# A two-layer transformer backbone on one core: the first and joining stages in another order, and a fourth size of expert, 65 to 96 rows

## The reference

```python
s_lat, s_ctx = silu(c), silu(c_ctx)
for layer in range(2):
    mod_l = split((s_lat @ ada_w[layer] + ada_b[layer]), 6)      # ada_w: 1024 x 6144, 25 MB a layer
    mod_c = split((s_ctx @ ada_w[layer] + ada_b[layer]), 6)
    hl = rmsnorm(xl, norm_g[layer, 0]) * (1 + mod_l[1]) + mod_l[0]   # hc likewise, with mod_c
    # layer 0: ab_mixer, h @ w_in (1024 x 3072), retention on four heads and a gated recurrence, @ w_out
    # layer 1: mla_mixer, latent attention of 16 heads
    xl = xl + mod_l[2] * ol
    tokens = rmsnorm(xl, norm_g[layer, 1]) * (1 + mod_l[4]) + mod_l[3]
    # router: one group of four, two of its eight experts; in layer 0 for all 768 tokens, in layer 1 for 512
    y = sum over the two experts e of  weight_e * ((silu(t @ w_gate[e]) * (t @ w_up[e])) @ w_down[e])
    xl = xl + mod_l[5] * y                                       # xc likewise, layer 0 only
return rmsnorm(xl, final_norm_g)
```

## Time and profile before

| | us |
|---|---|
| median of 3 runs | 2185.58 (2184.8 to 2187.6) |
| the profiled execution, own time | 2187.3 |
| its span in the profile | 2185.6 |
| PE busy | 1713.1 (78%) |
| DVE, ACT, POOL busy | 705.5, 435.5, 259.8 (32, 20, 12%) |
| mean granted TensorE clock | 0.899 |

### The profile page before, as it was taken

The page is one execution under the profiler, slowest core; times in us unless marked ns, Lnnn a source line. Parts: engine busy times, 40 slices in busy tenths (PEclk is TensorE's granted clock), DMA queues, the critical chain, the costliest instruction groups (busy, mean ns, idle before and its releaser), DMA issues. The chain is left out here.

```text
span 2185.6 us, 25873 instructions
## 1 busy us (share of the span) xinstructions
PE 1713.1 (78%) x9070; PEld 895.1 (41%) x9071; DVE 705.5 (32%) x1254; ACT 435.5 (20%) x802; POOL 259.8 (12%) x350
## 2 busy tenths in 40 slices
PE   5999999799499789998614899999938789855651
PEld 2443344645244334444303545555434334433330
DVE  2403675633311111112136227776331111111114
ACT  3102323311001110111113114554101101111112
POOL 1002350301100000001013110000111000000001
PEclk8999999899599999999865899999958999987885
DMA  9767653500799999999963002000169999999993
GB/s 320 239 246 250 217 175 120 199 26 39 315 385 361 413 418 412 424 398 403 419 269 123 2 0 87 1 1 8 54 254 389 414 410 406 413 413 410 414 413 137
DMA packets 105452, 568.10 MB, mean 260 GB/s; under 512 B 22728, under 2 KB 40904, under 8 KB 65568
## 3 DMA queue, kind: packets, MB, share of 16 engines
q1 hardware_dynamic: 90544, 521.94, 60.5%
q0 software_dynamic: 7744, 26.22, 3.4%
q10 hardware_dynamic: 7088, 18.92, 2.2%
HBM read 525.55 MB, written 41.50 MB: 259 GB/s over the span
## 5 line engine op out<-in xcount | busy, mean ns | idle before, releaser
L1927 PE MATMUL exp_gps<-moew_wg,all_hT 128*64 128x512 f32 (+1 forms) x480 | 238.6, 621 | 35.4 <-DMA moew_wu<-in_moe_w_up 33.1
L1921 PE MATMUL exp_gps<-moew_wg,all_hT 128*32 128x256 f32 x1088 | 160.5, 460 | 104.3 <-DMA moew_wu<-in_moe_w_up 97.9
L1928 PE MATMUL exp_ups<-moew_wu,all_hT 128*64 128x512 f32 (+1 forms) x480 | 237.3, 618 | 0.0
L583 PE MATMUL abp_ps<-ab_w,all_hT 128*128 128x512 f32 x384 | 169.6, 597 | 0.6 <-PE abp_ps L587 0.3
L1921 PE MATMUL exp_ups<-moew_wu,all_hT 128*32 128x256 f32 x1088 | 160.2, 460 | 0.0
L1921 PEld LDWEIGHTS exp_gps<-moew_wg,all_hT 128*32 128x32 f32 x1088 | 79.1, 131 | 182.5 <-issue 139.0
L1927 PEld LDWEIGHTS exp_gps<-moew_wg,all_hT 128*64 128x64 f32 (+1 forms) x480 | 77.7, 166 | 169.7 <-issue 169.7
L1955 PE MATMUL exp_yps<-moew_wd,all_hT 128*64 128x512 f32 (+1 forms) x240 | 117.3, 606 | 20.4 <-issue 20.4
L2047 DVE TENSOR_TENSOR all_hT<-all_hT,exp_ups 64x512 f32<-64x512 f32 (+1 forms) x30 | 20.7, 690 | 343.6 <-ACT all_hT L1997 343.6
L1957 PE MATMUL exp_yps<-moew_wd,all_hT 128*64 128x512 f32 (+1 forms) x240 | 116.8, 603 | 0.0
L583 PEld LDWEIGHTS abp_ps<-ab_w,all_hT 128*128 128x128 f32 x384 | 71.6, 190 | 98.5 <-issue 98.3
(11 more groups left out here) (399 smaller groups left out, 2572.0 us busy)
## 6 DMA issues: line engine op xcount, KB each, us to landing
moew_wg<-in_moe_w_gate SPq DMA_DIRECT2D x64, 2048.0 KB, 24.7
moew_wu<-in_moe_w_up SPq DMA_DIRECT2D x64, 2048.0 KB, 30.0
moew_wd<-in_moe_w_down SPq DMA_DIRECT2D x64, 2048.0 KB, 31.3
all_X<-in_ada_w SPq DMA_DIRECT2D x40, 1024.0 KB, 6.2
ab_w<-in_ab_w_in SPq DMA_DIRECT2D x6, 2048.0 KB, 9.1
ys<-abp_zero SPq DMA_DIRECT2D x32, 384.0 KB, 7.1
ys<-exp_y ACTq DMA_DIRECT2D x13, 512.0 KB, 8.7
ab_rows<-in_ada_w SPq DMA_DIRECT2D x6, 1024.0 KB, 12.0
```

Of the source, the lines that this page charges most:

```text
L583: last = nc.tensor.matmul(ps[i % RB][:], hT[:, kk, what * P:(what + 1) * P], w[n % S][:, kk, :], start=(kk == 0), stop=(kk == KD - 1))
L1921: last = nc.tensor.matmul(bank[lo + j * Q:lo + (j + 1) * Q, 0:HC], x[:, k, 0:Q], wt[:, k, j * HC:(j + 1) * HC], start=(k == 0), stop=(k == ...
L1927: nc.tensor.matmul(gps[0:rows, :], x[:, k, 0:rows], w.g[q][:, k, :], start=(k == 0), stop=(k == KD - 1))
L1928: last = nc.tensor.matmul(ups[at:at + rows, :], x[:, k, 0:rows], w.u[q][:, k, :], start=(k == 0), stop=(k == KD - 1))
```

## The change

It has three parts; nothing else is touched.

**The first stage** (`ab_project`). The six loads of rows go to the head of SP's queue, ahead of the chunks. The gains, convolution weights and biases, gate biases and lambdas come as 52 contiguous rows of 128 values (`laid`, five loads on ACT's queue); PE transposes them once and DVE copies them to columns (`pcols`). Block 0 is issued ahead of the tables. The transposes of the tiles stand behind earlier chunks. The ring has three buffers, and its uses move from two, two, two, one and one behind consecutive groups to one, two, two, two and one.

**The joining stage** of layer 0 is a new function, `combine_into_mla`: ACT scales the rows into `xn`, PE transposes them, ACT copies to `hT`, and gain and shift are applied to `hT` by columns, odd channels by ACT, even by DVE. POOL only issues gathers. Its modulation comes as five sets of eight rows (`laid`), transposed by PE. `combine` stays for the end of layer 1.

**The experts** get a form for 65 to 96 rows (`T3`): 64 rows in column halves and 32 rows in four column groups, each step with both. The 32 rows' gate and up are in a bank `qps`, their product in `h2`, their y in the bank `hps`. Gathers and stores of such an expert move 96 rows. The waits of PE for the copies of y (`y_act`, `y_dve`) stand, for all forms, ahead of the transposes of h and no longer behind them.

```diff
-        RING = 2
+        RING = 3
...
-        ADA_AT = [2 + 7 * r + r // 4 + at for r in range(ROUNDS - 1) for at in (0, 0, 1, 1, 2, 2, 3, 4)]
+        ADA_AT = [2 + 7 * r + r // 4 + at for r in range(ROUNDS - 1) for at in (0, 1, 1, 2, 2, 3, 3, 4)]
...
+            load_rows(sp, c, a, x_in)
             for kk in range(KD):
                 ada_chunk(0, kk, ada_first[kk], first_ready[kk])
+            block_of(0)
             tables.sync(sp)
-            block_of(0)
             block_of(1)
-            for t in range(CONV):
-                sp.dma_start(cw[:, t, :], a["lru_conv_w"][0, t].rearrange("(c p) -> p c", p=P),
-                             allow_slow_non_contiguous=True).then_inc(p_ready, 16)
-            sp.dma_start(cw[:, CONV, :], a["lru_conv_b"][0].rearrange("(c p) -> p c", p=P),
-                         allow_slow_non_contiguous=True).then_inc(p_ready, 16)
-            for dg in range(4):
-                sp.dma_start(gb[:, dg, :], a["lru_gate_b"][0, dg // 2, dg % 2].rearrange("(c p) -> p c", p=P),
-                             allow_slow_non_contiguous=True).then_inc(p_ready, 16)
+            sp.wait_ge(scaled, NT)
+            for n in range(RING):
+                ring_chunk(n)
             sp.dma_start(cs[:], a["ret_cs"]).then_inc(cs_ready, 16)
-            sp.wait_ge(scaled, NT)
-            ring_chunk(0)
-            ring_chunk(1)
             sp.wait_ge(gw_zero, 1)
...
-            after = {2: (0,), 3: (1,), 4: (2,), 5: (3, 4), 6: (5,)}
+            after = {0: (0, 1), 1: (2,), 2: (3,), 3: (4,), 4: (5,)}
+            pe.wait_ge(p_ready, 16 * 5)
+            nc.tensor.transpose(laid_cols, laid[:], c.ident[0:NL, 0:NL]).then_inc(laid_tr, 1)
             pe.wait_ge(silu_done, 1)
...
-            load_rows(act, c, a, x_in)
+            act.dma_start(laid[0:NG, :], a["norm_g"][0, 0].rearrange("(k p) -> k p", p=P)).then_inc(p_ready, 16)
+            act.dma_start(laid[NG:NW, :], a["lru_conv_w"][0].rearrange("t (c p) -> (t c) p", p=P)).then_inc(p_ready, 16)
+            act.dma_start(laid[NW:NC, :], a["lru_conv_b"][0].rearrange("(c p) -> c p", p=P)).then_inc(p_ready, 16)
+            act.dma_start(laid[NC:NB, :], a["lru_gate_b"][0].rearrange("d g (c p) -> (d g c) p", p=P)).then_inc(p_ready, 16)
+            act.dma_start(laid[NB:NL, :], a["lru_lambda"][0].rearrange("d (c p) -> (d c) p", p=P)).then_inc(p_ready, 16)
...
+            dve.wait_ge(laid_tr, 1)
+            V.tensor_copy(pcols[:], laid_cols).then_inc(cols_set, 1)
...
             with eng.If(rows > H):
-                work(P)
+                with eng.If(rows > T3):
+                    work(P)
+                with eng.Else():
+                    work(T3)
...
+                    if rows == T3:
+                        for k in range(KD):
+                            nc.tensor.matmul(gps[0:H, :], x[:, k, 0:H], w.g[q][:, k, :], start=(k == 0), stop=(k == KD - 1))
+                            nc.tensor.matmul(ups[H:P, :], x[:, k, 0:H], w.u[q][:, k, :], start=(k == 0), stop=(k == KD - 1))
+                            for wt, lo in ((w.g[q], 0), (w.u[q], H)):
+                                for j in range(2):
+                                    last = nc.tensor.matmul(qps[lo + j * Q:lo + (j + 1) * Q, :], x[:, k, H:T3],
+                                                            wt[:, k, j * HC:(j + 1) * HC],
+                                                            start=(k == 0), stop=(k == KD - 1))
+                        last.then_inc(gu_used, 1)
+                        return
...
+                    if rows == T3:
+                        for k in range(HT_N):
+                            nc.tensor.transpose(hps[:, k, 0:H], h_by[H:P, k // 2, k % 2, :], c.ident[H:P, H:P])
+                        for k in range(2):
+                            last = nc.tensor.transpose(hps[:, k, H:P], h2_by[H:P, k, :], c.ident[H:P, H:P])
...
-                    pe.wait_ge(y_act, n + 1)
-                    pe.wait_ge(y_dve, n + 1)
+                    if rows == T3:
+                        for k in range(HT_N):
+                            nc.tensor.matmul(yps[0][0:H, :], hT[:, k, 0:H], w.d[q][:, k, 0:512],
+                                             start=(k == 0), stop=(k == HT_N - 1))
+                            nc.tensor.matmul(yps[1][H:P, :], hT[:, k, 0:H], w.d[q][:, k, 512:1024],
+                                             start=(k == 0), stop=(k == HT_N - 1))
+                            for j in range(4):
+                                last = nc.tensor.matmul(hps_rows[j * Q:(j + 1) * Q, 0:HC], hT[:, k, H:T3],
+                                                        w.d[q][:, k, j * HC:(j + 1) * HC],
+                                                        start=(k == 0), stop=(k == HT_N - 1))
+                        last.then_inc(d_used, 1)
+                        return
...
                 pe.wait_ge(h_done, n + 2)
                 pe.wait_ge(ht_done, n + 1)
+                pe.wait_ge(y_act, n + 1)
+                pe.wait_ge(y_dve, n + 1)
...
+                        nc.scalar.activation(sg2[H:P, :], qps[0:H, :], ACT.Silu)
+                        nc.scalar.activation(sg[H:P, :], gps[0:H, :], ACT.Silu).then_inc(sg_done, 1)
...
+                            nc.scalar.copy(y[q][H:T3, j * HC:(j + 1) * HC], hps_rows[j * Q:(j + 1) * Q, 0:HC])
+                        nc.scalar.copy(y[q][0:H, 0:512], yps[0][0:H, :]).then_inc(y_act, 1)
...
+                        nc.vector.tensor_tensor(h2[H:P, :], sg2[H:P, :], qps[H:P, :], ALU.mult)
+                        nc.vector.tensor_tensor(h[H:P, :], sg[H:P, :], ups[H:P, :], ALU.mult).then_inc(h_done, 1)
...
+                        nc.vector.tensor_copy(hT[:, :, 0:H], hps[:, :, 0:H])
+                        nc.vector.tensor_copy(hT_by[:, :, :, H:T3],
+                                              hps[:, 0:2, H:P].rearrange("p b (a r) -> p b a r", a=2)).then_inc(ht_done, 1)
...
+def combine_into_mla(nc, c, a, r, prefetch):
...
+            for st in range(2):
+                sp.dma_start(laid[2 * st * KD:(2 * st + 2) * KD, :],
+                             c.mods[st, 1, 0:2 * DM].rearrange("(k p) -> k p", p=P)).then_inc(laid_ready, 16)
+            sp.dma_start(laid[4 * KD:, :], a["norm_g"][1, 0].rearrange("(k p) -> k p", p=P)).then_inc(laid_ready, 16)
+            load_gates(sp, c, gate, gate_ready, layer, 1, 2)
+            sp.wait_ge(got[0], 32)
+            prefetch(sp)
...
+            for t in range(T):
+                if t >= YB:
+                    pool.wait_ge(x_done, t - YB + 1)
+                for k in range(2):
+                    nc.gpsimd.indirect_dma_start(y[t % YB][k][:], None, c.ys[:, :],
+                                                 bass.IndirectOffsetOnAxis(r.slot[:, k * T + t:k * T + t + 1], 0)
+                                                 ).then_inc(got[t % YB], 16)
...
+            def weigh(t):
+                act.wait_ge(got[t % YB], 32 * (t // YB + 1))
+                nc.scalar.mul(y[t % YB][0][:], y[t % YB][0][:], r.w[:, 0, t:t + 1]).then_inc(weighed, 1)
+
+            def scale(t):
+                act.wait_ge(rstd_done, t + 1)
+                if t >= 2:
+                    act.wait_ge(tr, 2 * (t - 2) + 2)
+                nc.scalar.mul(xn[t % 2][:], c.X[:, t, :], norm.rstd[:, t:t + 1]).then_inc(scaled, 1)
+
+            def evict(t):
+                for half in range(2):
+                    act.wait_ge(tr, 2 * t + half + 1)
+                    nc.scalar.copy(c.hT[:, 4 * half:4 * half + 4, t * P:(t + 1) * P], tp[2 * (t % 2) + half][:]).then_inc(ev_act, 1)
+
+            def by_columns(half):
+                st, o, m = PARTS[half]
+                act.wait_ge(cols_done, 2)
+                act.wait_ge(ev_act, 2 * (o + m) // P)
+                for kk in range(1, KD, 2):
+                    nc.scalar.activation(c.hT[:, kk, o:o + m], c.hT[:, kk, o:o + m], ACT.Identity,
+                                         scale=cols[:, 2 * st + 1, kk:kk + 1], bias=cols[:, 2 * st, kk:kk + 1]).then_inc(aff, 1)
+
+            weigh(0)
+            weigh(1)
+            for t in range(T):
+                norm.square(act, t)
+                if t >= 1:
+                    scale(t - 1)
+                if t >= 2:
+                    evict(t - 2)
+                if t + 2 < T:
+                    weigh(t + 2)
+                if t == T - 1:
+                    by_columns(0)
+            scale(T - 1)
+            evict(T - 2)
+            evict(T - 1)
+            by_columns(1)
...
+            def inverse(t):
+                norm.inverse(dve, link, t)
+                dve.sem_inc(rstd_done, 1)
...
+            for t in range(T):
+                st = 1 if t < CT else 0
+                y0, y1 = y[t % YB]
+                dve.wait_ge(weighed, t + 1)
+                link(V.scalar_tensor_tensor(out=y0[:], in0=y1[:], scalar=r.w[:, 1, t:t + 1], in1=y0[:],
+                                            op0=ALU.mult, op1=ALU.add))
```

(9 more changed lines are left out.)

131 lines of the change are left out of this document (107 added, 24 removed).

## The result

| | us |
|---|---|
| before, median | 2185.19 (2182.76 to 2187.6, 4 runs) |
| changed, median | 2590.97 (2585.97 to 2601.91, 4 runs) |
| changed / before | 1.186 (95% interval 1.182 to 1.191) |
| predicted | 2138 (2123 to 2154) |

The changed kernel is 19% slower, where 2% faster was forecast. The profiled execution has a span of 2599.8 us, 414.2 more than before.

What follows compares the result with a forecast made beforehand. Loads bound the start and both expert stages, PE the projection, a chain of small steps the joining stage. 22.7 + 14.5 + 10.5 = 47.7 us off 2187.3, and 1.7 less beside the median, gave 2138 us (2123 to 2154).

Steps and rivals of the forecast that it cites:

- experts part: Both expert stages: fewer bytes and partly filled dry spells from the 96-row form, together 10.5 us less.
- Rival (4): Experts: a step's six matmuls run one after another, 3.4 us a step instead of 1.72; 2230 us, chance 0.02.
- Start: Before the projection: rows load first, block 0 lands last, first projection at 38.5 instead of 47.3, 8.8 us less.
- Ring waits: Projection: a third buffer cuts PE's 12.3 us of waits for chunks to 1.5, 10.8 us less.
- Clock: Projection: work slowed by the low clock that waits cause takes half at 1.00, 5.6 us less.
- 2.5 back at the start: Projection start: some low clock after PE stands nearly idle for block 0, 2.5 us more (0 to 7).
- First stage: Start and projection together: 8.8 + 10.8 + 5.6 - 2.5 = 22.7 us less (12 to 28).
- Joining stage: Between the expert layers: tiles at 5 us and an earlier PE start, 14.5 us less (9 to 18).
- Experts, 7.0 less for bytes: Expert stages: 11 experts gather and store 96 rows instead of 128, 0.64 us each, 7.0 us less.
- Experts, 3.5 less for dry spells: First expert layer: faster 96-row experts return buffers sooner, half of 7 us empty load time goes, 3.5 us less.
- Rival (5): Experts: no expert has 65 to 96 rows, so 10.5 us are missing; 2149 us, chance 0.02.

Runs made afterwards that it cites:

- t3_never: Changed kernel with the 96-row form's code in place on every engine but never taken, those experts running as 128 rows: 2586.15 us.
- no_t3: Changed kernel without the 96-row form, so 65 to 128 rows all run as 128 rows: 2156.28 us, 0.987 of before.
- t3_small: Changed kernel with experts of up to 32 rows on the 64-row form's matmuls, the 32-row form's code gone from PE, ACT and DVE: 2194.3 us.
- split0: Changed kernel without the 96-row form, waits for y in their old place, block 0 of the projection weights as two loads: 2152.6 us.
- p96: Changed kernel with experts of 65 to 96 rows computed by the 128-row form, only their gathers and stores cut to 96 rows: 2158.4 us, 0.989 of before.
- shared: Changed kernel with PE's 64-row and 32-row matmuls standing once each, an expert of 65 to 96 rows running both: 2159.3 us, 0.988 of before.

## Why the prediction was wrong

**The step that failed** is the pricing of the experts part. It counted what each executed instruction costs and never how many instructions the loop holds; the price of the added code was put at nothing, without a reason. It measured about 430 us (t3_never against no_t3). "The nearest rows" were sought for passes, changes and copies; that 72 matmuls and 6 transposes more in a branch make some 300 instructions more, three times over, in a loop that until then ran without a load of code, was in no term and no rival. Rival (4), the only slow one, had another mechanism (the six matmuls of a step one after another), and t3_small refutes it: its up step takes 12.7 us, where eight steps of 3.4 would be 27. (Its sum has a slip: beside 522 us of loads and 439 of work PE has 83 us free, not 73, so it would decide from 15 us an expert on, not 14.) The rows that spoke were there before the run: 48 packets on queue 8 in all, none from 660 to 1080 us.

**Start, 8.8 us less:** 7.1 measured (47.3 to 40.2). The order of events was right, block 0 came last, but it landed at 39.97, 1.5 us later than put: the last chunk landed at 34.6 instead of 33.4, and the block 5.4 behind it. The work behind the last chunk was put at 3.6 us; in split0 it took until 39.4, 4.9 behind a chunk that landed at 34.5. The last step on the chunks, at the lower clock, takes 1.9 us of it, where the earlier trace rows has 1.06. So block 0 came last by less than 1 us.

**Ring waits, 10.8 less:** 7.9 measured (12.3 to 4.4). One wait of 4.0 us remains, up to 127.8, and around it a stretch of 6.8 us at the lower clock (126.2 to 133.0).

**Clock, 5.6 less, and 2.5 back at the start:** together 1.8 less, from 379.8 - 363.0 = 16.8 in all minus 7.1 and 7.9. The 5.6 were worked out from the work at a clock of 0.50 in the stretch of the earlier trace rows and in one from 124.8 to 131.6 us. One of the two stayed (126.2 to 133.0 now, 0.50), and the start has one of its own from 34.0 to 44.3 (0.50), which reaches 4 us into the projection. First stage: 16.8 for a forecast of 22.7, inside its 12 to 28.

**Joining stage, 14.5 less:** 16.4 measured. The sums of the fourth to the sixth tile, in the changed kernel, answer to the earlier trace rows:

```profile
1366.79 1.23 DVE L2469 TENSOR_TENSOR all_X<-all_X,comb_y 128x1024 f32<-128x1024 f32 x1
1371.77 1.22 DVE L2469 TENSOR_TENSOR all_X<-all_X,comb_y 128x1024 f32<-128x1024 f32 x1
1376.75 1.22 DVE L2469 TENSOR_TENSOR all_X<-all_X,comb_y 128x1024 f32<-128x1024 f32 x1
```

They stand 4.98 us apart, as put (4.9 to 5.0, before 8.1). From the sixth sum's end at 1378.0 to the first latent matmul at 1391.0 it is 13.0 us, where 13.8 and 1.5 to give back had been put.

**Experts, 7.0 less for bytes:** nothing (p96). The share of DMA time of 1.00 in the earlier trace rows was read as time per byte. The runs show that it is not: with 1.9 MB less the same stage took the same time. What sets it then stays open; the waits for gathers and the pace of the weights' own queue were not separated.

**Experts, 3.5 less for dry spells:** nothing. The up step was sized right (12.7). Left out was the lower clock behind the waits around the down step, which makes the turn 25.9 us against 24.1; at the full clock it is 23.2, 0.9 less than 24.1, where 1 to 2 less was put. With the changes grouped and a short loop (shared) the empty time in the driest 10 us falls to 3.3 us (5.9 in no_t3, 5.0 in the earlier trace rows), so part of the spell is filled, as forecast, but the stage does not shrink. Either empty DMA time is not time of the stage, as the prediction took it to be, or the slower other forms of shared took it back; which of the two stays open.

Without the form the kernel takes 2152 to 2156 us. Rival (5) had put 2149 for a change that has the first two parts alone; that its figure comes near is in part luck, with 5.9 us too much in the first stage and 1.9 too little in the joining stage.
